# First layer's shift: weight rows scaled in place by ScalarE and summed by GpSimd in place of products on TensorE

## The chip, the cores and the metric

One core of a Trainium2 chip runs the whole program. The metric is the device time of one execution in microseconds. The engines are named as in the profile: PE is TensorE (PEld its weight load), DVE VectorE, ACT ScalarE, POOL GpSimd, SP SyncE, which only issues transfers; a name with a q behind it is that engine's own queue (issuing transfers, waiting).

## The reference, cut to what matters

The reference is two transformer-like blocks in float32 over 512 tokens of width 2048: two layers of a state-space mixer beside differential attention, then one layer of a gated delta rule beside sliding-window attention. Each layer begins with a normalisation that is modulated by a vector `c`:

```python
c_act = silu(c)                        # 2048
mod = c_act @ w_ada[l] + b_ada[l]      # w_ada[l]: 2048 x 6144
shift, scale, gate = split(mod, 3)
h = rms_norm(x, norm_g[l]) * (1 + scale) + shift
proj = h @ w_in[l]                     # its first columns are u
```

The case is about `shift` (2048 columns) of the first layer, l = 0.

## The kernel before, in words

**Plan.** `build` first writes one list of steps, `plan`, by Python generators (from line 396). Then each engine's function (`tensor`, `vector`, `scalar`, `gpsimd`, `sync`) walks the same list and emits its own part of each step. So every engine works in the order of the plan, and an engine that waits in one step holds all that stands behind it. Buffers come from first-in first-out rooms (`Room`, line 174): `take` hands out the place that has been free longest, `leave` records who must have finished with it, and the next tenant waits for that (`clear`). `temps` are 14 tiles of 128x512 in SBUF (`tring`), `aux` and `banks` the eight PSUM banks, `aslots` four places of 1 MB for the first layer's modulation weights: two halves of `yaT`, `SS` and `side`, memory that later stages use otherwise. `own()` makes an instruction wait for its engine's previous one.

**The start** (`start`, lines 532 to 604). x arrives and is turned by TensorE into `region_a`; the vectors are turned too, and ScalarE makes `cact`, silu(c) laid out as 128 partitions by 16 columns, one column for each 128 rows of `w_ada`. ScalarE and VectorE square x (`norm_square`), TensorE sums the squares. Then follow four **blocks** j = 0 to 3, each for 512 of the 2048 columns of scale and of shift. In a block there are four **pieces** k0 = 0, 4, 8, 12 of each: 4 times 128 rows by 512 columns, 1 MB. Pieces are fetched by SP (`first_fetch`, line 2984) in the order scale, shift, scale, shift, four ahead, and then one for each place given back; one 1 MB piece of `w_in` for `u` per block stands between them (`load_group`). In a block:

- `first_sum` (line 1729): VectorE multiplies the four 128x512 tiles of a scale piece by their columns of `cact` and adds them up in `acc` (one `tensor_scalar` at the very first, else `scalar_tensor_tensor` with the tile and `acc` in SBUF).
- `first_row` (line 1289): TensorE multiplies a column of `cact` by each 128x512 tile of a shift piece and adds up in one row of a PSUM bank: four products a piece, each of which the trace shows as two records.
- between the pieces, one step of the dense product for `u` on the previous block's `h` (`step_group`, `mm`): four products of 128x512.
- in block 0, `norm_root` (ScalarE's square root, VectorE's reciprocal) and `x_store`, ScalarE's 4 MB store of x.
- `norm_scale`: VectorE multiplies four tiles of x by the reciprocal root.
- `first_keep` (line 2478): ScalarE copies the row from PSUM to SBUF.
- `first_turn` (line 1300): TensorE turns `acc`, summing over its 128 partitions against a column of ones, and turns the row, into eight columns of the `mod` bank.
- `first_out` (line 1743): VectorE adds the bias and writes `mod`; then `norm_shift` (line 2534): ScalarE makes `h`, four tiles, with scale and bias from `mod`.
- then one part of the state-space preparation (`state_space_params`): after block 0 `ssm_fetch`, 14 transfers that ScalarE issues, in small rows (line 2581); after block 1 `prm_turn` and part 0 of `ssm_params`, small operations of VectorE on 128x32; after block 2 part 1 of it, with sines on ScalarE; after block 3 the last part.

After block 3 come a fence, the last quarter of the product for `u`, and the fence `start`, behind which GpSimd begins to fetch and to work. GpSimd has nothing to do in the start. Fences record each engine's latest signal.

Of the kernel before, what the change touches and what calls it, by code (L numbers as in the profile page):

```python
# [12 lines left out]
ACT = mybir.ActivationFunctionType  # L13
AX = mybir.AxisListType.X

P = 128
D = 2048
T = 512
KT = D // P
# [220 lines left out]
def build(nc, d, out, at, ncols):  # L240
    ctx = ExitStack()
    with ctx:
# [124 lines left out]
        squared = sem("squared", act)  # L367
        rooted = sem("rooted", act)
        h_ready = sem("h_ready", act)
        taken_a = sem("taken_by_act", act)  # L370
        ssm_a = sem("ssm_by_act", act)
        att_a = sem("attention_by_act", act)
# [25 lines left out]
        def do(*step):  # L398
            plan.append(step)
# [132 lines left out]
        def start():  # L532


            todo = [(part, j, k0) for j in range(4) for k0 in range(0, KT, 4) for part in (SCALE, SHIFT)]

            def fetch():
                if todo:
                    c = todo.pop(0)
                    aslots.take("first", *c)  # L540
                    do("first_fetch", *c)

            def turn_x(j):
# [24 lines left out]
            for j in range(4):  # L568
                temps.take("acc", 0, j)
                load_group(group, j)  # L570
                aux.take("row", j)
                temps.take("arow", j)
                steps_ = step_group(group, j - 1) if j else iter(())
                for k0 in range(0, KT, 4):
                    do("first_sum", j, k0)
                    aslots.give("first", SCALE, j, k0)
                    fetch()
                    do("first_row", j, k0)
                    aslots.give("first", SHIFT, j, k0)
                    fetch()  # L580
                    next(steps_, None)
                run_all(steps_)
                if j == 0:
                    temps.take("r", 0)
                    do("norm_root", 0)
                    aux.give("norm", 0)
                    do("x_store", 0)
                for k in range(4 * j, 4 * j + 4):
                    do("norm_scale", 0, k)
                do("first_keep", j)  # L590
                aux.give("row", j)
                do("first_turn", j)
                temps.give("acc", 0, j)
                temps.give("arow", j)
                do("first_out", j)
                for k in range(4 * j, 4 * j + 4):
                    do("norm_shift", 0, k)
                next(prep, None)
            aux.give("mod", 0)
            temps.give("r", 0)  # L600
            do("fence", "h", 0)
            run_all(step_group(group, 3))
            do("fence", "start")
            return prep
# [627 lines left out]
        def tensor():  # L1232
# [53 lines left out]
                i.then_inc(*ada_turned.up(m, n0))  # L1286
                temps.leave(("acc", m, n0), pe.mine())

            def first_row(j, k0):
                bank, place = aux.at("row", j), aslots.at("first", SHIFT, j, k0)  # L1290
                if k0 == 0:
                    room(aux.clear("row", j))
                pe.wait_ge(*att_a.of("silu"))
                pe.wait_ge(*first_landed(SHIFT, j, k0).of(SHIFT, j, k0))
                for k in range(k0, k0 + 4):
                    i = pe.matmul(bank[0:1, :], cact[:, 0, k:k + 1], place[:, k - k0, :], start=k == 0, stop=k == KT - 1)
                i.then_inc(*ada_turned.up("row", j, k0))
                aslots.leave(("first", SHIFT, j, k0), pe.mine())

            def first_turn(j):  # L1300
                bank, acc, row = aux.at("mod", 0), temps.at("acc", 0, j), temps.at("arow", j)
                if j == 0:
                    room(aux.clear("mod", 0))
                    pe.wait_ge(*d_ones.of())
# [1 line left out]
                for n in range(4):  # L1306
                    c = KT + 4 * j + n
                    pe.matmul(bank[:, c:c + 1], acc[:, n * P:(n + 1) * P], ones[:, 0:1], start=True, stop=True)
                pe.wait_ge(*taken_a.of("row", j))
                for n in range(4):  # L1310
                    c = 4 * j + n
                    i = pe.matmul(bank[:, c:c + 1], row[0:1, n * P:(n + 1) * P], ones[0:1, 0:1], start=True, stop=True)
                i.then_inc(*ada_turned.up("first", j))
                temps.leave(("acc", 0, j), pe.mine())
                temps.leave(("arow", j), pe.mine())

            def norm_square(l, k):
                if k == 0:
# [298 lines left out]
            def o_turn(j, k0):  # L1617
# [3 lines left out]
                for k in range(4):  # L1621
                    i = pe.transpose(bank[:, k * P:(k + 1) * P], regions[1][:, k0 + k, j * P:(j + 1) * P], ident)
                i.then_inc(*turned.up("o", j, k0))

            steps = dict(mm=mm, vec_turn=vec_turn, x_turn=x_turn, ada_turn=ada_turn, first_row=first_row, first_turn=first_turn,
                         norm_square=norm_square, norm_sum=norm_sum, prm_turn=prm_turn, root_sum=root_sum, u_turn=u_turn,
                         c_turn=c_turn, e_turn=e_turn, drive=drive, lags=lags, add_up=add_up, y_turn=y_turn, scores=scores,
                         w_turn=w_turn, values=values, band=band_, gate_sums=gate_sums, d_decay=d_decay, d_beta=d_beta, d_kk=d_kk,
# [791 lines left out]
        def scalar():  # L2420
# [54 lines left out]
                        *x_ready_a.up(j, k0))  # L2475
                    aux.leave(("x_turn", j, k0), act.mine())

            def first_keep(j):
                room(temps.clear("arow", j))
                act.wait_ge(*ada_turned.of("row", j, KT - 4))  # L2480
                act.activation(temps.at("arow", j)[0:1, :], aux.at("row", j)[0:1, :], ACT.Copy).then_inc(*taken_a.up("row", j))
                aux.leave(("row", j), act.mine())

            def sum_square(name, l, n):
                first_one = n == 0
# [320 lines left out]
            def o_turn(j, k0):  # L2806
                if k0 % 8:
# [3 lines left out]
                    act.activation(row[:, k0 * P:(k0 + 4) * P], aux.at("o_turn", j, k0)[:, :], ACT.Copy).then_inc(*taken_a.up("o", j, k0))  # L2811
                    aux.leave(("o_turn", j, k0), act.mine())

            steps = dict(rope=rope, norm_square=norm_square, norm_root=norm_root, x_store=x_store, norm_shift=norm_shift, norm_roots=norm_roots,
                         vec_fetch=vec_fetch, vec_turn=vec_turn, x_turn=x_turn, first_keep=first_keep, sum_square=sum_square,
                         root_square=root_square, root_sum=root_sum, u_turn=u_turn, keep_za=keep_za, save_zs=save_zs,
                         ssm_fetch=ssm_fetch, ssm_params=ssm_params, sine=sine, e_place=e_place, e_turn=e_turn, drive=drive,
                         bc_place=bc_place, gelu=gelu, soften=soften, w_turn=w_turn, glu_gate=glu_gate,
# [9 lines left out]
        def gpsimd():  # L2828
# [8 lines left out]
            def ada_fetch(m, n0, k):  # L2837
# [2 lines left out]
                room(mslots.clear("ada", m, n0, k))  # L2840
                pool.dma_start(mslots.at("ada", m, n0, k)[:, 0, :], w[k * P:(k + 1) * P, n0:n0 + 512]).then_inc(
                    *ada_landed(m, n0, k).landing("ada", m, n0, k))

            def ssm_clear(l):
                m = lay[l]
# [101 lines left out]
            def band_fetch():  # L2947
                room(passed("delta"))
                pool.wait_ge(*band_out.all())
                for h in range(16):  # L2950
                    pool.dma_start(band[:, h, :], bass.AP(band_dram.tensor, h * P * SW_W + 127, [[SW_W - 1, P], [1, 256]])).then_inc(
                        *band_in.landing())

            steps = dict(ada_fetch=ada_fetch, powers=powers, angles=angles, bc_place=bc_place, lags=lags, rotate=rotate, band=band_,
                         d_qd=d_qd, band_fetch=band_fetch, fence=fence_of(pool))
            for kind, *a in plan:
                if kind in steps:
# [124 lines left out]
```

## Time and profile before

| what | value |
|---|---|
| median of 3 runs | 4688.14 us (4687.24 to 4689.46) |
| the profiled execution's own time | 4688.89 us |
| its span in the profile | 4687.1 us |
| mean granted clock of TensorE | 0.97 of full speed |
| busy: TensorE, VectorE, ScalarE, GpSimd | 94%, 41%, 17%, 10% of the span |
| mean DMA rate | 106 GB/s |

The median stands 0.75 us under the profiled execution, whose own time is 1.8 us more than its span. Busy time says how long an engine had an instruction at work. The windows view gives it for a stretch of the span; the timeline lists instructions in order of time, with the idle time before one in brackets and what ended it. An instruction's time on an engine includes what it waits for once issued, so the same operation can show two durations.

### The profile page before, as it was taken

To read this page: it belongs to the slowest core of one execution; us is meant where nothing else is said; L and a number is where in the kernel's file an instruction comes from. 1 tells how busy PE (TensorE), PEld (TensorE's weight loads), DVE (VectorE), ACT (ScalarE), POOL (GpSimd) and SP (SyncE) were. 2 spreads that over 40 slices of the span, in tenths; PEclk is the share of its full clock that TensorE was granted. 3 is DMA by queue.
4 is the path that set the end of the run, shared out by engine and by line. 5 is a ranking of instruction groups with operands and counts; after the bars stand their busy time and mean duration, and the time that the engine had idled before them with its cause. 6 is when DMAs were issued, how large, how long until landed. Compare 5 with 4: busy or idle time off the path is not lost.

```text
span 4687.1 us, 34250 instructions
## 1 busy us (share of the span) xinstructions
PE 4429.2 (94%) x13238; PEld 2253.4 (48%) x13238; DVE 1940.2 (41%) x3496; ACT 818.5 (17%) x1384; POOL 484.1 (10%) x802
## 2 busy tenths in 40 slices
PE   7898899999889989999999899989899999999999
PEld 3454444444436545444444355555555554444444
DVE  4555535664543454356545535151514223321100
ACT  1122201231002221011300212120211013330000
POOL 0122211111321231101022000000000000000000
PEclk8999999999999999999999989999999999999999
DMA  8422233335472222322357321211121222223332
GB/s 295 171 90 74 92 109 104 115 120 169 151 239 79 86 72 83 110 88 68 108 190 233 127 81 36 69 49 59 47 70 48 92 72 68 67 88 128 99 103 76
DMA packets 366736, 495.17 MB, mean 106 GB/s; under 512 B 43899, under 2 KB 277870, under 8 KB 365550
## 3 DMA queue, kind: packets, MB, share of 16 engines
q1 hardware_dynamic: 288112, 340.16, 22.1%
q0 software_dynamic: 37632, 122.71, 8.2%
q10 hardware_dynamic: 40830, 30.11, 2.0%
q8 instruction: 105, 1.72, 0.1%
q14 instruction: 57, 0.47, 0.0%
HBM read 460.42 MB, written 32.51 MB: 105 GB/s over the span
## 4 chain that ended last, share of the span: by engine, by line
PE 75%; DVE 13%; DMA 6%; ACT 2%; issue 2%; ACTq 1%; POOL 0%; DVEq 0%; SPq 0%; POOLq 0%
PE bank L108 73%; DMA side<-in_w_ada 5%; DVE tring L123 4%; DVE tring L117 2%; PE bank L111 2%; ACT tring L114 1%; ACTq L147 1%; DVE tring L132 1%; DVE tring L120 1%; DVE CA L117 1%; DVE SS L117 1%; DVE tring L144 1%; DVE tb L117 1%; DVE dring L120 0%; ACT Est L114 0%
## 5 line engine op out<-in xcount | busy, mean ns | idle before, releaser
L108 PE MATMUL bank<-region_b,wring 128*128 128x512 f32 x4160 | 1872.5, 601 | 9.7 <-ACT region_b L114 9.7
L108 PEld LDWEIGHTS bank<-region_b,wring 128*128 128x128 f32 x4160 | 780.6, 193 | 904.6 <-issue 895.9
L108 PE MATMUL bank<-region_a,wring 128*128 128x512 f32 x2048 | 914.1, 601 | 10.8 <-DMA wring<-in_w_out 10.8
L108 PEld LDWEIGHTS bank<-region_a,wring 128*128 128x128 f32 x2048 | 387.8, 193 | 475.1 <-issue 473.7
L123 DVE SCALAR_TENSOR_TENSOR tring<-side,cact,tring 128x512 f32<-128x512 f32 x420 | 343.2, 817 | 218.1 <-DMA side<-in_w_ada 184.2
L147 POOL DMA_DIRECT2D side<-in_w_ada x448 | 242.8, 542 | 1499.2 <-DVE tring L123 976.5
L114 ACT ACT_TABLE_LOAD x196 | 251.5, 1283 | 437.9 <-DVE sring L120 285.4
L108 PE MATMUL bank<-wring,region_b 128*128 128x512 f32 (+2 forms) x768 | 285.4, 527 | 0.0
L132 DVE RECIPROCAL tring<-tring 128x512 f32<-128x512 f32 x54 | 180.7, 3348 | 134.1 <-ACT tring L114 134.0
L108 PE MATMUL bank<-wring,region_a 128*128 128x512 f32 x512 | 226.4, 600 | 5.9 <-ACT region_a L114 5.9
L108 PE MATMUL bank<-yaT,wring 128*128 128x512 f32 x512 | 227.3, 597 | 0.0
L108 PEld LDWEIGHTS bank<-wring,region_b 128*128 128x128 f32 x768 | 177.0, 253 | 104.1 <-issue 75.0
L108 PE MATMUL bank<-mixed,wring 128*128 128x512 f32 x512 | 219.9, 592 | 0.0
L117 DVE TENSOR_TENSOR tring<-bank,side 32x512 f32<-32x512 f32 (+1 forms) x160 | 110.0, 688 | 184.2 <-PE bank L108 180.3
L108 PEld LDWEIGHTS bank<-wring,region_a 128*128 128x128 f32 x512 | 126.6, 250 | 98.3 <-issue 68.8
L108 PEld LDWEIGHTS bank<-yaT,wring 128*128 128x128 f32 x512 | 98.2, 192 | 123.5 <-issue 123.5
L114 ACT ACTIVATE tring<-bank 128x512 f32<-128x512 f32 (+2 forms) x94 | 54.3, 578 | 590.1 <-PE bank L108 460.4
L108 PEld LDWEIGHTS bank<-mixed,wring 128*128 128x128 f32 x512 | 97.3, 190 | 122.5 <-issue 122.5
L114 ACT ACTIVATE region_a<-bank 128x512 f32<-128x512 f32 x48 | 28.0, 598 | 660.2 <-PE bank L111 449.7
L108 PE MATMUL bank<-dring,tring 128*128 128x128 f32 x704 | 107.4, 293 | 32.0 <-DVE tring L117 32.0
L117 DVE TENSOR_TENSOR tring<-tring 128x512 f32<-128x512 f32 (+2 forms) x142 | 96.9, 682 | 87.3 <-ACT tring L114 82.9
L114 ACT ACTIVATE tring<-bank,sring 128x128 f32<-128x128 f32 (+3 forms) x128 | 67.2, 526 | 375.8 <-DVE sring L120 375.6
(237 smaller groups left out, 3320.7 us busy)
## 6 DMA issues: line engine op xcount, KB each, us to landing
wring<-in_w_in SPq DMA_DIRECT2D x180, 1024.0 KB, 5.2
side<-in_w_ada POOLq DMA_DIRECT2D x448, 256.0 KB, 3.2
wring<-in_w_out SPq DMA_DIRECT2D x48, 1024.0 KB, 7.4
yaT<-in_w_ada SPq DMA_DIRECT2D x16, 1024.0 KB, 7.2
wring<-in_w_glu SPq DMA_DIRECT2D x16, 1024.0 KB, 7.8
tring<-x_saved SPq DMA_DIRECT2D x48, 256.0 KB, 3.6
SS<-in_w_ada SPq DMA_DIRECT2D x8, 1024.0 KB, 8.3
side<-in_w_ada SPq DMA_DIRECT2D x8, 1024.0 KB, 9.1
```

The costliest lines, as they stand in the source:

```text
L108: return self.e.matmul(*a, **k) if self.e else self
L111: return self.e.transpose(*a) if self.e else self
L114: return self.e.activation(*a, **k) if self.e else self
L117: return self.e.tensor_tensor(*a) if self.e else self
L120: return self.e.tensor_scalar(*a) if self.e else self
L123: return self.e.scalar_tensor_tensor(out=o, in0=a, scalar=s, in1=b, op0=op0, op1=op1) if self.e else self
L132: return self.e.reciprocal(*a) if self.e else self
L144: return self.e.tensor_tensor_scan(*a) if self.e else self
L147: return self.e.dma_start(dst, src, allow_slow_non_contiguous=True) if self.e else self
```

## The change

The shift's pieces are no longer multiplied on TensorE. A new step `first_shift` takes the place of `first_row`: ScalarE multiplies each of a piece's four 128x512 tiles by its column of `cact`, in place in the piece's slot (`activation` Copy with a column as scale), and signals each tile. GpSimd adds the tiles up in `shift_acc`, a 128x512 tile of `temps` that takes the place of `arow`: 15 `tensor_tensor` additions a block, each waiting for the scaled tile and for GpSimd's previous one. The piece's place is given back by GpSimd's last addition, no longer by TensorE's last product. `first_turn` waits for GpSimd's sum and turns its 128 partitions against ones, as it does with `acc`. The PSUM bank of the row and the copy `first_keep` are gone. ScalarE's part of `first_shift` stands in its order where the plan has the piece: before `norm_root` and `x_store` in block 0, before `norm_shift` in all blocks, and after the preparation's part of the block before.

```diff
@@ start
                 load_group(group, j)
-                aux.take("row", j)
-                temps.take("arow", j)
+                temps.take("shift_acc", j)
...
-                    do("first_row", j, k0)
+                    do("first_shift", j, k0)
                     aslots.give("first", SHIFT, j, k0)
...
-                do("first_keep", j)
-                aux.give("row", j)
                 do("first_turn", j)
...
@@ tensor
-            def first_row(j, k0):
...
-                for k in range(k0, k0 + 4):
-                    i = pe.matmul(bank[0:1, :], cact[:, 0, k:k + 1], place[:, k - k0, :], start=k == 0, stop=k == KT - 1)
-                i.then_inc(*ada_turned.up("row", j, k0))
-                aslots.leave(("first", SHIFT, j, k0), pe.mine())
...
-                pe.wait_ge(*taken_a.of("row", j))
+                pe.wait_ge(*shift_ready.of(j))
                 for n in range(4):
                     c = 4 * j + n
-                    i = pe.matmul(bank[:, c:c + 1], row[0:1, n * P:(n + 1) * P], ones[0:1, 0:1], start=True, stop=True)
+                    i = pe.matmul(bank[:, c:c + 1], shift[:, n * P:(n + 1) * P], ones[:, 0:1], start=True, stop=True)
@@ scalar
-            def first_keep(j):
...
+            def first_shift(j, k0):
+                place = aslots.at("first", SHIFT, j, k0)
+                act.wait_ge(*first_landed(SHIFT, j, k0).of(SHIFT, j, k0))
+                own()
+                for k in range(k0, k0 + 4):
+                    act.activation(place[:, k - k0, :], place[:, k - k0, :], ACT.Copy, scale=cact[:, 0, k:k + 1]).then_inc(*scaled.up(j, k))
@@ gpsimd
+            def first_shift(j, k0):
+                acc, place = temps.at("shift_acc", j), aslots.at("first", SHIFT, j, k0)
+                for k in range(max(k0, 1), k0 + 4):
+                    pool.wait_ge(*scaled.of(j, k))
+                    if k == 1:
+                        room(temps.clear("shift_acc", j))
+                    own()
+                    pool.tensor_tensor(acc, place[:, 0, :] if k == 1 else acc, place[:, k - k0, :], AD).then_inc(
+                        *(shift_ready.up(j) if k == KT - 1 else g_step.up()))
+                aslots.leave(("first", SHIFT, j, k0), pool.mine())
```

## Rows read from the trace of the kernel before

A piece is named by block and first tile, as (2,8); columns `[N <- who]` are idle time before.

**Rows 1.** The page's busy time (us, share of the span, instructions).
```profile
PE 4429.2 (94%) x13238; PEld 2253.4 (48%) x13238; DVE 1940.2 (41%) x3496; ACT 818.5 (17%) x1384; POOL 484.1 (10%) x802
```

**Rows 2.** Windows, start and rest (last columns: granted clock, DMA share, GB/s).
```profile
0.00:188.80 188.80, 147.06 (x405) 68.42 (x406) 90.56 (x207) 28.28 (x44) 0.20 (x4) 0.90 0.76 271
...
188.80:4687.10 4498.30, 4282.12 (x12835) 2184.95 (x12833) 1849.68 (x3290) 790.21 (x1342) 483.91 (x798) 0.97 0.31 99
```

**Rows 3.** Timeline: TensorE in blocks 2 and 3 (start us, us, engine, line, operation).
```profile
127.41 5.29 PE L108 MATMUL bank<-yaT,cact 128*1 128x512 f32 x8 [4.33 <-DMA yaT<-in_w_ada]
...
136.38 3.59 PE L108 MATMUL bank<-side,cact 128*1 128x512 f32 x8
...
143.57 1.93 PE L108 MATMUL bank<-ones,tring 128*128 128x1 f32 x16
```

**Rows 4.** Timeline: VectorE's first write of the modulation, ends of blocks 0 to 3.
```profile
65.23 0.22 DVE L117 TENSOR_TENSOR mod<-bank,vec 128x4 f32<-128x4 f32 x2
...
104.79 0.23 DVE L117 TENSOR_TENSOR mod<-bank,vec 128x4 f32<-128x4 f32 x2 [17.42 <-PE bank L108]
...
145.53 0.23 DVE L117 TENSOR_TENSOR mod<-bank,vec 128x4 f32<-128x4 f32 x2 [10.09 <-PE bank L108]
...
186.84 0.23 DVE L117 TENSOR_TENSOR mod<-bank,vec 128x4 f32<-128x4 f32 x2 [10.01 <-PE bank L108]
```

**Rows 5.** Timeline: ScalarE's queue in block 1, and the row's copy behind it.
```profile
67.95 12.31 ACTq L147 DMA_DIRECT2D Bn<-in_ssm_b_im  x1
...
99.68 2.53 ACTq L147 DMA_DIRECT2D tring<-in_ssm_c_im  x4
...
102.26 0.59 ACT L114 ACTIVATE tring<-bank 1x512 f32<-1x512 f32 x1 [33.64 <-issue]
```

**Rows 6.** Timeline: ScalarE's four scalings with column operands.
```profile
105.25 2.93 ACT L114 ACTIVATE region_b<-region_b,mod 128x512 f32<-128x512 f32 x4 [2.41 <-DVE mod L123]
```

**Rows 7.** Timeline: squares, first sums, root and reciprocal in block 0; VectorE's scaling.
```profile
23.34 4.26 ACT L114 ACTIVATE tring<-region_a 128x512 f32<-128x512 f32 x8
...
28.34 2.33 DVE L123 SCALAR_TENSOR_TENSOR tring<-yaT,cact,tring 128x512 f32<-128x512 f32 x3
...
39.46 0.69 ACT L114 ACTIVATE tring<-bank,const 128x512 f32<-128x512 f32 x1
...
59.43 3.35 DVE L132 RECIPROCAL tring<-tring 128x512 f32<-128x512 f32 x1
...
132.95 2.49 DVE L117 TENSOR_TENSOR region_b<-region_a,tring 128x512 f32<-128x512 f32 x4
```

**Rows 8.** Tile view: GpSimd's 128x512 additions (ns minimum/median/maximum).
```profile
L117 POOL TENSOR_TENSOR q<-tring x16: 1253/1257/1803, 617.8 to 2207.8; 128x512 f32<-128x512 f32 x16
```

**Rows 9.** Timeline: GpSimd and VectorE at work together.
```profile
253.67 1.04 POOL L117 TENSOR_TENSOR tring<-r,const 128x512 f32<-128x512 f32 x1 [6.24 <-DVE SS L117]
...
253.69 1.57 DVE L123 SCALAR_TENSOR_TENSOR tring<-side,cact,tring 128x512 f32<-128x512 f32 x1
...
254.79 1.37 POOL L117 TENSOR_TENSOR tring<-th,const 128x512 f32<-128x512 f32 x1
```

**Rows 10.** Timeline and DMA view (us to landing) of pieces in blocks 2, 3.
```profile
119.79 0.92 SPq L147 DMA_DIRECT2D yaT<-in_w_ada  x2
...
161.00 0.92 SPq L147 DMA_DIRECT2D yaT<-in_w_ada  x2
...
yaT<-in_w_ada SPq DMA_DIRECT2D x1, 1024.0 KB, 5.0
...
side<-in_w_ada SPq DMA_DIRECT2D x1, 1024.0 KB, 9.1
```

**Rows 11.** DMA view: us to landing at 38; ScalarE queue's share, 65.6 to 104.5.
```profile
x_saved<-region_a ACTq DMA_DIRECT2D x1, 4096.0 KB, 17.2
...
q10 hardware_dynamic: 12640, 1.61, 27.8%
```

**Rows 12.** Busy time of VectorE in its parameter step after block 1.
```profile
106.60:116.90 10.30, 8.68 (x48) 0.80 0.00 0
```

More of the change, by code:

```diff
@@ L369, in build @@
         h_ready = sem("h_ready", act)
+        scaled, shift_ready = sem("scaled_by_act", act), sem("shift_ready", pool)
         taken_a = sem("taken_by_act", act)
@@ L589, in start @@
                     do("norm_scale", 0, k)
-                do("first_keep", j)
-                aux.give("row", j)
                 do("first_turn", j)
                 temps.give("acc", 0, j)
-                temps.give("arow", j)
+                temps.give("shift_acc", j)
                 do("first_out", j)
@@ L1287, in ada_turn @@
                 temps.leave(("acc", m, n0), pe.mine())
-            def first_row(j, k0):
[L1290 to L1294, printed above, removed]
-                for k in range(k0, k0 + 4):
-                    i = pe.matmul(bank[0:1, :], cact[:, 0, k:k + 1], place[:, k - k0, :], start=k == 0, stop=k == KT - 1)
-                i.then_inc(*ada_turned.up("row", j, k0))
-                aslots.leave(("first", SHIFT, j, k0), pe.mine())
             def first_turn(j):
-                bank, acc, row = aux.at("mod", 0), temps.at("acc", 0, j), temps.at("arow", j)
+                bank, acc, shift = aux.at("mod", 0), temps.at("acc", 0, j), temps.at("shift_acc", j)
                 if j == 0:
@@ L1308, in first_turn @@
                     pe.matmul(bank[:, c:c + 1], acc[:, n * P:(n + 1) * P], ones[:, 0:1], start=True, stop=True)
[L1309 removed]
+                pe.wait_ge(*shift_ready.of(j))
                 for n in range(4):
                     c = 4 * j + n
[L1312 removed]
+                    i = pe.matmul(bank[:, c:c + 1], shift[:, n * P:(n + 1) * P], ones[:, 0:1], start=True, stop=True)
                 i.then_inc(*ada_turned.up("first", j))
                 temps.leave(("acc", 0, j), pe.mine())
[L1315 removed]
+                temps.leave(("shift_acc", j), pe.mine())
             def norm_square(l, k):
@@ L1623, in o_turn @@
                 i.then_inc(*turned.up("o", j, k0))
-            steps = dict(mm=mm, vec_turn=vec_turn, x_turn=x_turn, ada_turn=ada_turn, first_row=first_row, first_turn=first_turn,
+            steps = dict(mm=mm, vec_turn=vec_turn, x_turn=x_turn, ada_turn=ada_turn, first_turn=first_turn,
                          norm_square=norm_square, norm_sum=norm_sum, prm_turn=prm_turn, root_sum=root_sum, u_turn=u_turn,
@@ L2476, in x_turn @@
                     aux.leave(("x_turn", j, k0), act.mine())
-            def first_keep(j):
[L2479 to L2482, printed above, removed]
+            def first_shift(j, k0):
[4 more added lines that the diff above has]
+                    act.activation(place[:, k - k0, :], place[:, k - k0, :], ACT.Copy, scale=cact[:, 0, k:k + 1]).then_inc(*scaled.up(j, k))
             def sum_square(name, l, n):
@@ L2812, in o_turn @@
                     aux.leave(("o_turn", j, k0), act.mine())
-            steps = dict(rope=rope, norm_square=norm_square, norm_root=norm_root, x_store=x_store, norm_shift=norm_shift, norm_roots=norm_roots,
-                         vec_fetch=vec_fetch, vec_turn=vec_turn, x_turn=x_turn, first_keep=first_keep, sum_square=sum_square,
+            steps = dict(first_shift=first_shift, rope=rope, norm_square=norm_square, norm_root=norm_root, x_store=x_store, norm_shift=norm_shift, norm_roots=norm_roots,
+                         vec_fetch=vec_fetch, vec_turn=vec_turn, x_turn=x_turn, sum_square=sum_square,
                          root_square=root_square, root_sum=root_sum, u_turn=u_turn, keep_za=keep_za, save_zs=save_zs,
@@ L2952, in band_fetch @@
                         *band_in.landing())
-            steps = dict(ada_fetch=ada_fetch, powers=powers, angles=angles, bc_place=bc_place, lags=lags, rotate=rotate, band=band_,
+            steps = dict(first_shift=first_shift, ada_fetch=ada_fetch, powers=powers, angles=angles, bc_place=bc_place, lags=lags, rotate=rotate, band=band_,
                          d_qd=d_qd, band_fetch=band_fetch, fence=fence_of(pool))
```

## The prediction

> **What bounds the kernel now.** The page's busy times come first: TensorE works 94% of the span [rows 1]. The windows view splits that: after 188.8 us TensorE is 95% busy, and before, in the first layer's start, 78%, while the DMA engines carry 271 GB/s [rows 2]. All edits lie in the start. Nothing behind it refers to absolute time (loads, fetches and fences all follow the start's last step), so what the start gains or loses passes on one to one, and the start must be read step by step. The time shown for the profiled execution is 4688.9 us (span 4687.1), 0.8 above the median of 4688.1; I sum against it and move the result by the same amount.
>
> Blocks 2 and 3 end on TensorE: after piece (2,8) of the shift has landed come row products 5.3 us, products of `u` 3.8, row products 3.6, `u` 3.8, turning 1.9 [rows 3], and VectorE writes the modulation at 145.5. Block ends are 65.2, 104.8, 145.5 and 186.8 [rows 4]. Block 1 ends on ScalarE: its queue issues parameter loads from 65.7 to 102.2, and the copy of the row, behind them, runs at 102.3 [rows 5].
>
> **What goes.** 64 row products (128 records): 16 pieces by about 3.6 us, 58 us of TensorE, which is mostly cover, not path. Per block 2 and 3 two of them stand in the closing chain. The four row copies and the one-partition turning go too; the new turning has as many instructions. No DMA is added or removed; loads keep their order on SP, but a shift piece's place comes free only when GpSimd has added it, and SP is in order, so every later load queues behind it. I price that below.
>
> **Prices of what comes.** ScalarE scales a 128x512 tile by a column in 0.73 us (2.93 for four) [rows 6]. That is a bias too, so an upper bound; the squares give 0.53 (4.26 for eight) as the lower [rows 7]. I take 0.73, the same operand kind. GpSimd adds two full tiles in 1.26 at the least [rows 8]; I take 1.34 with the gap between its dependent instructions (from 253.67+1.04 to 254.79 is 0.08 [rows 9]). There are 15 additions per block, and ScalarE keeps ahead of them.
>
> The price that decides is what both engines cost each other. Where GpSimd works on SBUF, VectorE's two-input sum takes 1.57 us, ending 0.55 after GpSimd's addition, and GpSimd's next one 1.37 where it takes 1.04: +0.33 [rows 9]. Alone a sum takes 0.78 (2.33 for three) [rows 7]. So while both have work they alternate, a pair in 1.26+0.08+0.33 = **1.67 us**. Bounds: 1.34 for the pair (no hindrance) and 2.1 (no overlap at all, 1.26+0.08+0.78). The Trainium skill, page "SBUF — State Buffer", section "Who interferes with whom", says that a VectorE instruction with two SBUF inputs and a GpSimd one that reads SBUF exclude each other, the loser waiting for the whole instruction. By whole instructions the pair would cost 2.1, some 10 us more in all over the 24 pairs; the rows show exclusion, but with GpSimd's start-up hidden, so they decide.
>
> **Block 0.** ScalarE's squares end at 27.6, VectorE's sums start at 27.8 [rows 7]. After two scalings (1.5) GpSimd starts at 29.1: seven additions at 1.67 end at 40.8, and the place for the last shift piece is free. It lands by 46.5 (5 to 9 us from issue [rows 10]), ScalarE scales it to 49.4; only then comes the root, behind it in program order, some 2 us (table and 0.69 [rows 7]), and the 4 MB store of x leaves at **51.5**, not 38. VectorE: two sums clean, fourteen at 1.67, to 52.5; reciprocal 3.35 and scaling 2.5 [rows 7], modulation at 58.8. That is 6.4 earlier than 65.2, but the next block does not start from it.
>
> **Block 1.** ScalarE is now in front of the additions, and its 14 parameter loads stand before its first scaling. Call F the time they are issued. The store ahead in the same queue takes 17.2 to land; the parameters took 27.8% of 38.9 us of all engines, 10.8 [rows 11]; one 1 MB piece beside them 2.6 (of four pieces the first lands 5.0 after 119.8, the last, issued at 123.4, 9.1 later at 132.5: 7.7 over three [rows 10]). F = 51.5+17.2+10.8+2.6 = **82.1**. Bounds: 59.3+10.8 = 70.1 if the store does not matter, 59.3+36.5 = 95.8 if the issue takes as long as before [rows 5]. From F: scalings 1.5, three additions 4.0, four more 5.4, to F+10.9; piece 8, issued at F+5.6, is usable at F+11.9; then eight additions, one at 1.34 and seven at 1.67 (VectorE has four sums and then four scalings of the norm, two SBUF inputs each) to F+24.9; turning 1.1 (half of 1.93 and a handover), to F+26.4 with VectorE's queue. End 108.5 against 104.8: **+3.7**.
>
> **Blocks 2 and 3.** Before the first sum VectorE has its parameter step: 10.3 us, 48 small instructions of 0.2 [rows 12], nearly all on SBUF. (In block 3 the step has a stop for ScalarE's sines in it, behind which ScalarE's first scaling now queues; 12.6 us, priced alike.) GpSimd meanwhile adds the two pieces already there, seven additions, 9.5 us, starting some 5 to 7 us into the block. I let two small instructions, 3.1 us in 9.5, pass per addition: VectorE is 6.4 late. Bounds 0 (no hindrance) and 9.5 (none pass); the small operands are not shown beside a long addition, so I take a value between, nearer to the hindered row. The fetch of the next pieces, 15.0 and 15.5 us into the block [rows 4, 10], slips by the 6.4. From that issue the block took 25.7 (145.5-119.8). Now: the shift piece lands and is scaled at +8.5 (127.4-119.8 and 0.8), two additions 2.7, six at 1.67, 10.0, turning 1.1: 22.3. So -3.4+6.4 = **+3.0** in each, **+6.0**.
>
> **Behind.** TensorE idles for 20 us ahead of the dense products. Eight records after such a wait took 5.3 where warm ones take 3.6 [rows 3]: **+1.7**. Before, this was paid inside the block and the dense part started warm. Bounds 0 and 3.4. The row's PSUM bank leaves the rotation; nothing waits long on banks in the start, later order may shift: 0, bounds -3 and +3.
>
> Sum: 3.7+6.0+1.7 = **+11.4 us**: 4700.3 for the profiled execution, 4699.5 against the median.
>
> **Rivals.**
> A. *GpSimd and VectorE do not hinder each other here* (other tiles than in rows 11). Then the blocks 2 and 3 take 8.5+8x1.34+1.1 = 20.3 from issue, -5.4 each with nothing late; the last shift piece of block 0 is in two us earlier, F is 80, block 1 ends 0.9 early; with +1.7 the sum is -10.0: 4678. For: TensorE's closing chain really goes. Against: the 1.57 [rows 9], which is a sum of just this kind over tiles of just this size. 10%. This is the other side; it decides where a pair costs under 1.4.
> B. *ScalarE is held as long as before.* F = 95.8, the sum is +25: 4713. For: small descriptors and a full ring; against: SP, held by the shift places, leaves the DMA engines nearly free. 15%.
> C. *The loads drain fast* (F near 72) *or more small instructions pass*: +1: 4689, no change. 22%.
> My forecast has 50%; some 3% lie beyond all.
>
> **How the numbers follow.** What a measurement here can tell from none is about 0.2%, 9.4 us. The forecast's own spread, 4692 to 4708, lies on both sides of 4697.5, about 38 to 12. Slower: 38+15+2 = 55. Same: 12+22+2 = 36. Faster: 9. The range takes in C and B's point and part of A: 4683 to 4714.
>
> **What would show it.** In the changed kernel: VectorE's sums of 1.5 us and more wherever GpSimd adds; a parameter step of 15 us or more; x's store near 51; ScalarE's first scaling of block 1 near 82; block ends near 59, 108, 152, 196; TensorE idle before the dense products with the clock low. Sums staying at 0.78 would prove the hindrance wrong; F under 75 or over 90 moves block 1 alone.

## The result, and the profile after

The changed kernel takes **4703.43 us** (median of 7 runs, 4695.55 to 4707.78), the kernel before on the same chip 4688.14 (7 runs, 4685.52 to 4689.69). The ratio is 1.0031, 95% interval 1.0019 to 1.0043: 15.3 us slower, where the forecast was 11.4 slower. Every run of the changed kernel lies above every run of the kernel before. Slower was the likeliest case (0.55), and the time lies in the range. One of the six runs of a2_after_again, further down, took 14334.18 us; the median given there is that of the other five.

The page's busy times, to be set beside [rows 1]:

```profile
PE 4377.5 (93%) x13110; PEld 2248.0 (48%) x13110; DVE 1984.5 (42%) x3496; ACT 856.9 (18%) x1444; POOL 568.2 (12%) x862
```

TensorE lost 52 us of work and 128 records, as meant (64 products of two records each). VectorE executes the very same 3496 instructions, yet is busy 44 us longer. That is the first thing to see: nothing was added to VectorE, its instructions became longer. GpSimd got its 60 additions, 84 us for them.

The windows view, start and rest, as [rows 2]:

```profile
0.00:198.30 198.30, 90.65 (x271) 62.85 (x272) 134.98 (x206) 66.85 (x104) 84.09 (x64) 0.71 0.74 260
198.30:4703.30 4505.00, 4286.84 (x12841) 2185.17 (x12839) 1849.56 (x3291) 790.03 (x1342) 484.10 (x798) 0.97 0.31 98
```

All of the 44 us on VectorE lie in the start (135.0 against 90.6), as does TensorE's relief (90.7 against 147.1). The start is 9.5 us longer, although its formerly busiest engine is now idle for more than half of it.

VectorE's first write of the modulation, ends of blocks 0 to 3, as [rows 4]:

```profile
55.99 0.22 DVE L117 TENSOR_TENSOR mod<-bank,vec 128x4 f32<-128x4 f32 x2
...
106.10 0.23 DVE L117 TENSOR_TENSOR mod<-bank,vec 128x4 f32<-128x4 f32 x2 [0.81 <-PE bank L108]
...
151.03 0.23 DVE L117 TENSOR_TENSOR mod<-bank,vec 128x4 f32<-128x4 f32 x2 [0.81 <-PE bank L108]
...
196.37 0.23 DVE L117 TENSOR_TENSOR mod<-bank,vec 128x4 f32<-128x4 f32 x2 [0.80 <-PE bank L108]
```

The bracket changed as much as the time. Before, VectorE stood idle for 17, 10 and 10 us ahead of these writes, and TensorE ended the wait. Now it is idle for 0.8: VectorE is itself at work until just before the block's end (its last scaling in block 2 ends at 150.2, GpSimd's last addition at 149.1, and TensorE's turning of that sum stands between). The block lengths are 50.1, 44.9 and 45.3 us, against 39.6, 40.7 and 41.3.

What VectorE does in block 2, the timeline of the changed kernel:

```profile
110.62 0.19 DVE L117 TENSOR_TENSOR w<-w 128x32 f32<-128x32 f32 x1
110.85 0.18 DVE L120 TENSOR_SCALAR w<-w 128x32 f32<-128x32 f32 x1
111.07 1.25 DVE L117 TENSOR_TENSOR w<-w 128x32 f32<-128x32 f32 x1
112.35 0.18 DVE L120 TENSOR_SCALAR w<-w 128x32 f32<-128x32 f32 x1
112.56 1.17 DVE L117 TENSOR_TENSOR w<-w 128x32 f32<-128x32 f32 x1
...
115.39 1.16 DVE L120 TENSOR_SCALAR w<-prm 128x32 f32<-128x32 f32 x1
...
125.12 0.48 DVE L120 TENSOR_SCALAR tring<-yaT,cact 128x512 f32<-128x512 f32 x1
...
138.11 6.50 DVE L123 SCALAR_TENSOR_TENSOR tring<-SS,cact,tring 128x512 f32<-128x512 f32 x4 [1.97 <-DMA SS<-in_w_ada]
144.53 5.69 DVE L117 TENSOR_TENSOR region_b<-region_a,tring 128x512 f32<-128x512 f32 x4
```

and GpSimd in the same block:

```profile
111.00 1.27 POOL L117 TENSOR_TENSOR tring<-yaT 128x512 f32<-128x512 f32 x1 [6.86 <-ACT yaT L114]
112.41 2.70 POOL L117 TENSOR_TENSOR tring<-tring,yaT 128x512 f32<-128x512 f32 x2
115.25 5.50 POOL L117 TENSOR_TENSOR tring<-tring,side 128x512 f32<-128x512 f32 x4
136.38 6.01 POOL L117 TENSOR_TENSOR tring<-tring,yaT 128x512 f32<-128x512 f32 x4 [15.62 <-ACT yaT L114]
142.53 6.54 POOL L117 TENSOR_TENSOR tring<-tring,side 128x512 f32<-128x512 f32 x4
```

Read the two by the clock. At 111.00 GpSimd's first addition begins, and VectorE's next small instruction, at 111.07, takes 1.25 us where its like, 0.45 earlier, took 0.19. The parameter step now lasts 17.1 us for the same work, 10.3 before [rows 12]. At the block's other end four sums take 6.50 and four scalings of the norm 5.69, where 3.11 and 2.49 were usual, and four additions take 6.54 beside them, against 5.50 in the parameter step.

### The profile page after: what moved, and what is told of

Read it like the earlier page. It is cut to its first block, busy times and chain, and to the rows that moved or that the text cites. A ratio compares the mean times of both kernels' runs of the same rounds, so it can differ in the third digit from the quotient of the medians.

```text
span 4703.3 us, 34189 instructions
## 1 busy us (share of the span) xinstructions
PE 4377.5 (93%) x13110; PEld 2248.0 (48%) x13110; DVE 1984.5 (42%) x3496; ACT 856.9 (18%) x1444; POOL 568.2 (12%) x862
## 4 chain that ended last, share of the span: by engine, by line
PE 74%; DVE 14%; DMA 5%; ACT 3%; issue 2%; POOL 1%; ACTq 1%; DVEq 0%; SPq 0%; POOLq 0%
PE bank L108 72%; DMA side<-in_w_ada 5%; DVE tring L123 4%; DVE tring L117 2%; PE bank L111 2%; ACT tring L114 1%; POOL tring L117 1%; ACTq L147 1%; DVE tring L120 1%; DVE tring L132 1%; DVE CA L117 1%; DVE SS L117 1%; DVE tring L144 1%; DVE tb L117 1%; DMA yaT<-in_w_ada 0%
## 5 line engine op out<-in xcount | busy, mean ns | idle before, releaser
L108 PE MATMUL bank<-ones,tring 128*128 128x1 f32 x288 | 44.6, 276 | 116.5 <-DVE tring L123 108.1
L114 ACT ACTIVATE tring<-bank 128x512 f32<-128x512 f32 (+1 forms) x90 | 52.0, 578 | 471.4 <-PE bank L108 375.5
```

The costliest lines, as they stand in the source:

```text
L108: return self.e.matmul(*a, **k) if self.e else self
L114: return self.e.activation(*a, **k) if self.e else self
```

## The experiments

Eleven experiments with nine different kernels follow, in three groups. The members of a group (e1, e2, e3, v1; a2, e5, v2, v3; a3, e6, e4) share a chip and its runs of the kernel before, whose medians were 4684.20 (20 runs), 4686.27 (19) and 4688.33 (18). Differences below are against the median of the same group. Block ends are read as above.

| kernel | median us | ratio, 95% interval | ends of blocks 0 to 3 in its trace |
|---|---|---|---|
| e1_bank | 4696.18 | 1.0030 (1.0018 to 1.0042) | 57.9, 109.5, 154.4, 199.5 |
| e2_adds_alone | 4690.47 | 1.0015 (1.0005 to 1.0024) | 65.2, 103.2, 149.9, 194.9 |
| e3_short_adds | 4670.62 | 0.9970 (0.9958 to 0.9983) | 53.3, 96.1, 130.4, 165.5 |
| v1_u_early | 4672.32 | 0.9975 (0.9964 to 0.9986) | 63.7, 98.2, 139.1, 173.1 |
| a2_after_again | 4701.49 | 1.0029 (1.0017 to 1.0041) | 56.1, 107.2, 152.2, 197.6 |
| e5_loads_later | 4699.34 | 1.0027 (1.0017 to 1.0037) | 56.2, 90.8, 148.7, 194.0 |
| v2_block0_new | 4684.43 | 0.9994 (0.9984 to 1.0004) | 56.1, 102.2, 142.9, 184.1 |
| v3_both | 4669.94 | 0.9963 (0.9950 to 0.9975) | 55.9, 101.7, 135.1, 169.0 |
| a3_after | 4701.09 | 1.0032 (1.0020 to 1.0044) | 54.6, 105.8, 150.9, 196.1 |
| e6_bank_again | 4700.17 | 1.0027 (1.0016 to 1.0038) | 55.9, 105.9, 150.9, 196.3 |
| e4_adds_behind_params | 4692.22 | 1.0011 (1.0002 to 1.0020) | 55.7, 105.6, 147.3, 188.8 |

### The additions alone (e2_adds_alone)

The kernel before, with 15 additions a block that nobody needs, on a tile that is free in the start. TensorE keeps the row products.

```diff
                     do("first_row", j, k0)
+                    do("idle_adds", j, k0)
...
+            def idle_adds(j, k0):
...
+                pool.wait_ge(*first_landed(SHIFT, j, k0).of(SHIFT, j, k0))
+                for k in range(max(k0, 1), k0 + 4):
+                    own()
+                    pool.tensor_tensor(sinT[:, :], sinT[:, :], sinT[:, :], AD).then_inc(*g_step.up())
```

> The kernel before, its shift still on TensorE, plus 15 idle GpSimd additions per block of a 128x512 tile that nobody reads, started when ScalarE has made the block's h and the shift piece has landed. Theory A (hindrance): VectorE's parameter steps grow from 10.3 us to about 18, its sums beside an addition from 0.75 to over 1.5; blocks 2 and 3 take 47 to 48 us in place of 40.7 and 41.3, block 0 loses 0 to 4, in all 4702 to 4707 us, though no result of GpSimd is waited for. Theory C (the loss is the length of GpSimd's chain, which is waited for): no change, 4688 us, parameter step 10.3 us.

Measured: 6.3 us slower than the kernel before, where I had expected 14 to 19. Blocks 2 and 3 take 46.7 and 45.1 us, about as long as in the changed kernel. Timeline of VectorE in block 2:

```profile
120.55 0.48 DVE L120 TENSOR_SCALAR tring<-yaT,cact 128x512 f32<-128x512 f32 x1
...
133.47 5.08 DVE L123 SCALAR_TENSOR_TENSOR tring<-SS,cact,tring 128x512 f32<-128x512 f32 x4 [1.97 <-DMA SS<-in_w_ada]
138.48 5.01 DVE L117 TENSOR_TENSOR region_b<-region_a,tring 128x512 f32<-128x512 f32 x4
149.85 0.23 DVE L117 TENSOR_TENSOR mod<-bank,vec 128x4 f32<-128x4 f32 x2 [6.36 <-PE bank L108]
```

The first sum comes 17.35 us into the block, 12.1 before. Since these additions have nothing to do with the shift, the late parameter step belongs to GpSimd's being at work, not to the data or to ScalarE. At the end VectorE still waits 6.4 us for TensorE: the stretched sums cost nothing there. In this kernel the hindrance acts by the late fetch alone. The size was missed because blocks 0 and 1 lost nothing (block 1 even took 38.0 us, not 39.6), and because these additions, on one tile alone, are shorter (7.97 us for seven, 9.75 in the changed kernel), so that the parameter step takes 15.5 us and not 18.

### Short additions (e3_short_adds)

The changed kernel with additions over 64 of the 512 columns, all but each block's first. So 7/8 of the shift sums lack their later terms; every instruction, wait and transfer stays.

```diff
-                    pool.tensor_tensor(acc, place[:, 0, :] if k == 1 else acc, place[:, k - k0, :], AD).then_inc(
+                    n = T if k == 1 else 64
+                    pool.tensor_tensor(acc[:, 0:n], place[:, 0, 0:n] if k == 1 else acc[:, 0:n], place[:, k - k0, 0:n], AD).then_inc(
```

> The changed kernel with GpSimd's additions, but the first, over 64 of the 512 columns (7 of 8 shift sums then lack their later terms); count and waits stay. An addition then takes some 0.35 us. Both theory A and theory C expect the blocks to shorten: blocks 2 and 3 from 44.9 and 45.3 us to 33 to 35. A expects the parameter step back at 10.3 to 11.5 us, which is 7 of these 11 us per block, the rest from the closing chain; C expects the step as in the changed kernel and only the closing chain shorter, blocks of 40. In all: A 4670 to 4676 us, C 4688 to 4692.

Measured: 13.6 us *faster* than the kernel before, as theory A had it; blocks 2 and 3 take 34.3 and 35.1 us, and the parameter step after block 1 11.4. VectorE in block 2:

```profile
109.37 0.48 DVE L120 TENSOR_SCALAR tring<-yaT,cact 128x512 f32<-128x512 f32 x1
...
122.38 3.11 DVE L123 SCALAR_TENSOR_TENSOR tring<-SS,cact,tring 128x512 f32<-128x512 f32 x4 [1.97 <-DMA SS<-in_w_ada]
125.41 2.86 DVE L117 TENSOR_TENSOR region_b<-region_a,tring 128x512 f32<-128x512 f32 x4
130.40 0.23 DVE L117 TENSOR_TENSOR mod<-bank,vec 128x4 f32<-128x4 f32 x2 [2.13 <-PE bank L108]
```

The first sum is back at 13.3 us into the block and four sums at 3.11. So the relief of TensorE is real, and worth some 14 us: it is the *length* of the additions that turns this gain into 13 to 15 us of loss. Handovers, waits and ScalarE's scalings are all still there and are cheap. The run shortens GpSimd's own chain together with what the additions do to VectorE. In the parameter step e2_adds_alone separates the two. In the closing chain no run does: its eight additions took 12.7 us, and at the unhindered 1.37 apiece they would take 11.0 (an estimate from the rows above), so most of that chain is GpSimd's own length.

### Additions behind the parameter step (e4_adds_behind_params)

The changed kernel with one more wait: in blocks 2 and 3 GpSimd starts adding when VectorE has finished its parameter step.

```diff
             def first_sum(j, k0):
+                if j >= 2 and k0 == 0:
+                    after_params[j] = dve.mine()
...
+                if j >= 2 and k0 == 0:
+                    pool.wait_ge(*after_params[j])
                 for k in range(max(k0, 1), k0 + 4):
```

> The changed kernel with one more wait: in blocks 2 and 3 GpSimd begins its additions only when VectorE has reached the block's first sum, behind its parameter step. Theory 1 (the late parameter step is a cost of its own in those blocks): the step takes 10.3 to 10.8 us again and the first sum stands 12.1 to 12.6 after the block's start, not 19; seven additions now stand beside sums, in pairs of 1.64, so the last pieces are fetched some 24 us into the block and the block takes 38 to 43 us, not 45. Rival (GpSimd's and VectorE's time simply adds up over the whole block, wherever the additions stand): the block stays at 44 to 46 us. By the first the median is 4 to 12 us under a3_after, by the second within 2.

Measured: 8.9 us under the changed kernel on the same chip (a3_after), blocks 41.7 and 41.5 us; theory 1, in the middle of its range. Timeline of VectorE in block 2:

```profile
117.75 0.48 DVE L120 TENSOR_SCALAR tring<-yaT,cact 128x512 f32<-128x512 f32 x1
118.26 5.00 DVE L123 SCALAR_TENSOR_TENSOR tring<-yaT,cact,tring 128x512 f32<-128x512 f32 x3
123.36 6.57 DVE L123 SCALAR_TENSOR_TENSOR tring<-SS,cact,tring 128x512 f32<-128x512 f32 x4
130.03 4.00 DVE L123 SCALAR_TENSOR_TENSOR tring<-yaT,cact,tring 128x512 f32<-128x512 f32 x4
135.06 5.77 DVE L123 SCALAR_TENSOR_TENSOR tring<-SS,cact,tring 128x512 f32<-128x512 f32 x4 [1.03 <-DMA SS<-in_w_ada]
```

The first sum stands 12.1 us into the block (117.75 - 105.61), as before the change. Doing the additions *later* ends the block *earlier*. An addition costs VectorE about as much in either place, 0.87 beside a sum (1.65 instead of 0.78) and 1.0 beside a small instruction. But the parameter step stands ahead of the fetch, and what it loses is lost to all behind it; the sums stand beside transfers. In the changed kernel VectorE waited for these 1.85 and 1.97 us ahead of its last eight sums; here one such wait of 1.03 is left, and the last four sums begin 29.4 us (135.06 - 105.61) into the block and not 32.0 (138.11 - 106.10). One wait took the change from 1.0032 to 1.0011. So the late parameter step is a cost of its own, 3.3 and 3.8 us a block net of what moved.

### The parameter loads (e5_loads_later)

The changed kernel with the 14 loads behind block 1's scalings.

```diff
                 run_all(steps_)
+                if j == 1:
+                    next(prep, None)
...
-                next(prep, None)
+                if j:
+                    next(prep, None)
```

> The changed kernel with ScalarE's 14 parameter loads issued behind block 1's scalings (all pieces) in place of ahead of them. Theory A with my term for ScalarE's queue: block 1's additions start at some 61 us in place of 81.5, its sums end near 88 to 90, but block 1's h and the parameter step wait for the loads, which now go out at 80 to 98: the block's modulation is written at 90, the parameter step starts some 6 us earlier than in the changed kernel; blocks 2 and 3 unchanged; in all 6 us less, 4697 against 4703. Rival: the loads only move, and the parameter step waits for them as long as before or longer: 0 to +5 us.

Measured: 13.1 us slower than the kernel before, 2.2 under a2_after_again, where theory asked for 6. Block 1 ends at 90.8, 16.4 earlier than there, and block 2 gives 12.8 of it back. ScalarE's queue, and VectorE behind it:

```profile
99.48 2.20 ACTq L147 DMA_DIRECT2D tring<-in_ssm_c_im  x4
101.78 2.93 ACT L114 ACTIVATE region_b<-region_b,mod 128x512 f32<-128x512 f32 x4 [18.78 <-issue]
```

```profile
90.81 0.23 DVE L117 TENSOR_TENSOR mod<-bank,vec 128x4 f32<-128x4 f32 x2 [0.81 <-PE bank L108]
...
104.33 0.47 DVE L126 COPY tring<-tring 32x128 f32<-32x128 f32 x2 [13.09 <-DMA tring<-in_ssm_c_im]
```

The parameter step needs these loads. They hold ScalarE for 18.8 us here and for 20.7 in the changed kernel, and here the step waits 13.1 us for the last of them. So block 1 has two bounds close together, the scalings behind the loads and the loads themselves; lifting the first alone bought 2 to 4 us.

### The banks (e1_bank, e6_bank_again) and the changed kernel again (a2_after_again, a3_after)

```diff
                 temps.take("acc", 0, j)
                 load_group(group, j)
+                aux.take("row", j)
                 temps.take("shift_acc", j)
...
+                aux.give("row", j)
                 do("first_turn", j)
```

> The changed kernel with one difference: the PSUM bank that the shift's row used to hold is taken and given back as before, so that later stages get their banks in the old order. Theory A (all of the loss comes from the start, where GpSimd and VectorE hinder each other): no effect, 4703 us, and the modulation of block 3 is written near 196.4 us as in the changed kernel. Theory B (the 4 to 5 us that the changed kernel loses behind the start come from the changed order of banks): same start, but only some 11 us over the kernel before at the end, 4699 us.

> The changed kernel once more, unaltered, beside the others. Theory A: the start ends (modulation of block 3 written) within 3 us of 196.4, 9 to 13 us over the kernel before, and what the whole execution loses beyond that varies from run to run with no cause in the change: the time from there to the end, 4507 us in the first trace, lies anywhere in the 4490 to 4507 that the traces so far show. Theory B (a fixed loss behind the start): again 4505 us or more from there to the end.

> The changed kernel unaltered, a third time, to set the kernel with the bank beside it on one chip. If what the medians show beyond the start (about 4 us) belongs to the kernel and not to the single executions, the median is again 14 to 16 us over the kernel before. If it is scatter between executions and chips, it falls anywhere from 10 to 17. Block ends as before: 56, 106 to 107, 151 to 152, 196 to 198.

> The changed kernel with the row's PSUM bank taken and given back unused, so that every later step gets the bank it had before. Theory 1: the order of the banks is worth nothing; the median agrees with a3_after within 2 us. Theory 2: the order of the banks costs some 3 us behind the start; the median is 3 to 4 us under a3_after, though its start is as long.

The changed kernel came out at +15.3, +15.2 and +12.8 us on three occasions, with the bank at +12.0 and +11.8. By itself e1_bank looked like theory B, 12 over the kernel before in place of 15, but nothing unaltered ran beside it, and its start ended 3 us later than I had said (199.5, not 196.4). In the same group the two differ by 0.9 us (4701.09 and 4700.17): the order of the banks is worth nothing that shows. The time from block 3's end to the end of the span was 4500.3 us in the kernel before's trace, and 4506.9, 4501.0 and 4497.0 in the three of the changed kernel. So the first trace's 4506.9 does not come back. Whether a smaller loss stands behind the start is not settled. The trace of a3_after is that of its shortest run (4694.88), 6 us under its median. Over all traces, the eight in which GpSimd sums block 3's shift have 4497.0 to 4506.9, 4500.7 on average, and the five in which TensorE does have 4490.2 to 4500.3, 4496.1 on average. The cold clock that comes up below explains 1.2 to 2.2 us of this difference of 4.6; the rest is not clear of the scatter.

### Taking the other way: v1_u_early, v2_block0_new, v3_both

v1 is the kernel *before* with one edit. The closing chain of its blocks 2 and 3 holds two steps of `u`, 3.8 us each, that wait for nothing [rows 3]; they go ahead of the last pieces, into TensorE's idle time.

```diff
                     fetch()
-                    next(steps_, None)
+                    if k0 < 8:
+                        next(steps_, None)
+                        next(steps_, None)
```

> The kernel before with TensorE's four steps of the product for u placed beside a block's first two pieces (two steps each) in place of one beside each piece. In blocks 2 and 3 TensorE waits for the third piece anyway, so that 7.6 us of the closing chain should move into that wait: blocks of 33 to 34 us in place of 40.7 and 41.3, block 1 unchanged (ScalarE's queue ends it), 4674 us. Rival: the fetches, not TensorE, set these blocks once TensorE's chain is short, or TensorE is late for the first pieces and gives their places back later: 0 to -5 us, 4683 to 4688.

Measured: 11.9 us *faster* than the kernel before, near the 14 that I had expected, but not in the blocks that I had named. Block 3 takes 34.0 us, as expected. Timeline of TensorE at its end:

```profile
153.26 7.26 PE L108 MATMUL bank<-wring,region_b 128*128 128x512 f32 x16
162.35 3.59 PE L108 MATMUL bank<-yaT,cact 128*1 128x512 f32 x8 [1.83 <-DMA yaT<-in_w_ada]
167.53 3.59 PE L108 MATMUL bank<-side,cact 128*1 128x512 f32 x8 [1.58 <-DMA side<-in_w_ada]
171.05 2.03 PE L108 MATMUL bank<-ones,tring 128*128 128x1 f32 x16
```

The row products now wait for DMA, which bounds the block; TensorE is no longer late, and its clock stays up (3.59 for eight records). Block 2 took 40.9 us and gained nothing, since VectorE waited for `in_ssm_c_im`, as in e5. Block 1, which I had expected unchanged, took 34.5 us and not 39.6: the loads held ScalarE for 28.6 us and not 33.6, for a reason that no run shows. The hit of the total is in part luck.

```profile
95.65 0.59 ACT L114 ACTIVATE tring<-bank 1x512 f32<-1x512 f32 x1 [28.57 <-issue]
```

```profile
104.88 0.47 DVE L126 COPY tring<-tring 32x128 f32<-32x128 f32 x2 [6.26 <-DMA tring<-in_ssm_c_im]
```

v2 is block 0 of the changed kernel with blocks 1 to 3 of the one before (`NEW` is `(0,)`); v3 adds v1's edit to v2.

```diff
-                    do("first_shift", j, k0)
+                    do("first_shift" if j in NEW else "first_row", j, k0)
```

> Block 0 by ScalarE and GpSimd as in the changed kernel, blocks 1 to 3 by TensorE as before. Block 0 ends at 56 as in the changed kernel (65 before), the parameter loads start 9 us earlier, block 1 ends at 94 to 97 (104.8 before), blocks 2 and 3 take 40.7 and 41.3 as before: 8 to 10 us faster than before, 4679. Rival: the fetches of block 1, which the store of x now meets, set its end: 0 to -4 us.

> Block 0 as in the changed kernel, blocks 1 to 3 by TensorE, and the products for u in each block's first two pieces, as in v1_u_early. If both gains hold and add: 13.7 us (v1's start) and 8 to 10 us, in all 22 to 24 us faster than before, 4665. Rival: both shorten the way to the same wait, VectorE's for the parameter loads at some 104 us; then only 14 to 18 us.

v2: 1.8 us under the kernel before, an interval that holds no change; that is the rival's size, not the 8 to 10 us that I expected. Block 0 ends 9.1 us earlier, but block 1's row copy runs at 99.66 where it ran at 102.26 [rows 5]. The loads, begun earlier, meet the end of x's store (issued at 45.69, landed 22.0 later) and are held for 40 us instead of 34; that the store is the reason is argued, no run tests it.

```profile
62.04 18.90 ACTq L147 DMA_DIRECT2D Bn<-in_ssm_b_im  x1
80.97 16.41 ACTq L147 DMA_DIRECT2D tring<-in_ssm_c_re  x4
97.41 2.20 ACTq L147 DMA_DIRECT2D tring<-in_ssm_c_im  x4
99.66 0.59 ACT L114 ACTIVATE tring<-bank 1x512 f32<-1x512 f32 x1 [40.19 <-issue]
```

v3: 16.3 us faster than the kernel before, with blocks 2 and 3 at 33.4 and 33.9 us, so here both of the closing chains that v1 was to shorten are shorter. It beats both kernels and has the lowest ratio of all. Its gain is the rival's 14 to 18, not the 22 to 24 that I expected: as in v2, most of what block 0 gains is given back at the loads. Between v1 (0.9975) and v3 (0.9963) the intervals overlap.

## Why the prediction was right, step by step

The forecast was +11.4 us. In the traces the start's last step is 9.5, 10.8 and 9.3 us later in the three executions of the changed kernel, and the dense products behind it add 1.8, 2.2 and 2.2; so 11 to 13 us lie where I put them. The medians say 15.3, 15.2 and 12.8. The 1 to 4 us that are over have no cause that a run shows.

- **Block 0**: forecast end 58.8, measured 56.0. The price of a pair was right: 6.59 for four sums and 6.54 for four additions, **1.65 and 1.64** against my 1.67. Of the 2.8 us, 1.6 are the sums' earlier begin (26.25, against 27.83 before), which is no part of the change's mechanism. What I had wrong is the place of the store. I let the last shift piece be scaled at 49.4 and the store go at 51.5; it went at 45.66, 0.1 after the scaling of that piece's first tile began, with three scalings and the root still to come (the root ran at 49.42). The trace of the kernel before could have told me: there the root's table load ran at 38.16, the store was issued at 38.22, and the root itself ran at 39.46. A scaling costs 0.64 us in a row of four (2.56), not the 0.73 of [rows 6], where a bias is added as well.
- **Block 1**, forecast +3.7, measured +1.3 (106.1 against 104.8). F came out at 80.1, forecast 82.1. Two errors met: the store left 5.8 us earlier, but took 21.9 us to land and not 17.2 (26.0 and 26.2 in the other two traces of this kernel); that pieces fetched beside it are the reason is argued, not tested. From F to the end 26.0 us, forecast 26.4. The timeline of ScalarE:

```profile
45.66 0.41 ACTq L147 DMA_DIRECT2D x_saved<-region_a  x1
...
77.80 2.20 ACTq L147 DMA_DIRECT2D tring<-in_ssm_c_im  x4
80.11 2.56 ACT L114 ACTIVATE yaT<-yaT,cact 128x512 f32<-128x512 f32 x4 [20.73 <-issue]
```

- **Blocks 2 and 3**, forecast +3.0 each, measured **+4.2 and +4.0**. The parameter step makes VectorE 6.9 and 6.75 us late; I had 6.4, between 0 and 9.5. From the fetch to the block's end it takes 23.0 and 23.1; I had 22.3. The additions were right (6.01 and 6.54, and 8.4 ahead of them); the turning takes 1.86, where I had 1.1 with the handover, since TensorE comes to it after 20 us of idle time and its granted clock is 0.50 (1.2 GHz) in both of its stretches; before, at 1.00, sixteen records took 1.93 [rows 3]:

```profile
144.67 1.87 PE L108 MATMUL bank<-ones,tring 128*128 128x1 f32 x8 [20.83 <-DVE tring L123]
149.13 1.86 PE L108 MATMUL bank<-ones,tring 128*128 128x1 f32 x8 [2.60 <-POOL tring L117]
```

- **Cold clock**, forecast +1.7, measured +1.8 in the first execution. The windows view from block 3's end to the end of the dense products, the kernel before and then the changed one:

```profile
186.84:223.47 36.63, 36.53 (x98) 26.45 (x99) 25.25 (x64) 8.18 (x13) 13.18 (x21) 1.00 0.30 99
```

```profile
196.37:234.80 38.43, 38.43 (x98) 28.01 (x98) 25.25 (x64) 8.18 (x13) 13.18 (x21) 0.94 0.22 69
```

The same 98 records take 1.8 us longer, with the granted clock at 0.94 in place of full speed (2.4 GHz). TensorE comes out of 21.5 us of idle time at the lower level: 0.50 from 190.0 to 199.6, 1.00 from 205.0 on. The other traces agree: 37.8 to 38.9 us for this stretch wherever GpSimd sums block 3, 36.6 in all five where TensorE does.
- **Banks**, forecast 0: e6_bank_again.
- **Rival A** (no hindrance) fell: its condition was a pair under 1.4 (where it names rows 11, the row in question is in [rows 9]). e3_short_adds shows what it would have meant; there the change pays. **Rival B** (ScalarE held as long as before) fell with F = 80.1; its fear was sound in another place, since v2 shows the loads held for 40 us. x's store was under way in v2 and in the changed kernel alike, so it alone does not do that. The difference that the traces show is SP: in v2 it went on fetching, and the DMA engines moved 344 to 393 GB/s from 65 to 90; in the changed kernel the second of the two transfers shown here waited for a place until 85.6, and the rate fell to 201 and 182 GB/s between 70 and 80. That is the argument that I had set against B.

```profile
59.21 26.79 SPq L147 DMA_DIRECT2D yaT<-in_w_ada  x2
```

- **Rival C** fell on both conditions: F is not 72, and the small instructions pass more rarely than I let them.

The terms erred in both directions: block 1 by -2.4, blocks 2 and 3 together by +2.2, and the near hit of the sum is in part luck. The sign was not: the parameter step and the closing chain went as priced, and both prices hung on one row, the 1.57 us sum of [rows 9].

The seven additions in the parameter step cost VectorE 6.9 us, about one small instruction stretched by 1.0 for each, the two-input one at 111.07 to 1.25 us and the `TENSOR_SCALAR` at 115.39 to 1.16, while the additions kept their 1.37. The Trainium skill, page "SBUF — State Buffer", section "Who interferes with whom", has VectorE instructions with two SBUF inputs and GpSimd ones that read SBUF exclude each other, and an instruction with one SBUF input only in a two-port mode. The traces agree for two inputs, at 128x512 and at 128x32; the `TENSOR_SCALAR` was hit too, and in which mode it runs no trace shows. By whole instructions, as the page has it, a pair would cost 2.1 us (an estimate from the rows of either alone); it costs 1.64.

## What to carry to other kernels

Work that moves to an idle GpSimd is not free if VectorE works on SBUF at the same time: price each pair from a row where they overlap (1.64 us here, where the two alone add up to 2.1), and keep the long GpSimd instructions away from runs of small VectorE ones that stand ahead of a fetch, since each addition cost one such run a whole microsecond and one added wait took back 9 of 13. Before taking work off an engine whose last steps end a stage, look at which of them need not be last: moving two steps of `u` forward in each block gave 12 us (in its trace 7.3 in block 3, as meant, and 5.1 in block 1, where the loads held ScalarE for less), where moving the row products to two other engines cost 13 to 15.

## What the runs showed of the hardware that was not expected

- A pair of a 128x512 sum and a 128x512 addition costs 1.64 us, where alone a sum takes 0.78 and an addition 1.34 to 1.37 with its gap: 0.5 us of one is hidden behind the other.
- Small instructions (128x32) pay nearly the full length of the addition: 1.25 and 1.17 in place of 0.19.
- ScalarE's queue issued the 4 MB store at 45.66, though the root that stands ahead of it in program order ran at 49.42. In the kernel before it went at 38.22, with the root at 39.46. In both traces it left 0.1 us after the last wait ahead of it was over (the piece's landing, 45.55; the bank, 38.16), with the activations behind that wait still to run.
- The 4 MB store took 17.2 us to land in the kernel before and 21.9 to 26.2 in three traces of the changed one. The 14 small-row loads held ScalarE for 20.7 us in the changed kernel, where SP issued nothing from 60.0 to 85.6, for 28.6 in v1, 33.6 in the kernel before and 40.2 in v2.
